# All cached value pages weighed on TensorE in four groups of PSUM rows, and head sums made from high and low parts

## The reference

```python
q, k, v, u, vc = split(rmsnorm(h, g_mix) @ w_in)        # 8 heads of 128 each
q, k = rmsnorm(q, g_q), rmsnorm(k, g_k)                 # per head
vc = layernorm(gelu(vc)); u = gelu(u)                   # per channel group of 128
z = q . k / sqrt(128) + bias_h                          # stick-breaking attention
A[t, s] = sigmoid(z[t, s]) * prod(s < j < t, 1 - sigmoid(z[t, j]))
o_sb = A @ v                                            # for a sample: 1024 cached values and weights
o_cm = u * (tril(W_s) @ vc + b)
h += concat(rmsnorm(o_sb), rmsnorm(o_cm)) @ w_out
h += (silu(rmsnorm(h) @ w_gate) * (rmsnorm(h) @ w_up)) @ w_down
h += sigmoid(rmsnorm(h) @ w_ple_gate) * (p @ w_ple_proj)
```

## Time and profile before

| | |
|---|---|
| median of 3 runs | 2385.37 us (2383.94 to 2385.87) |
| the profiled execution's own time | 2386.52 us |
| its span, first to last instruction | 2384.8 us |
| mean granted TensorE clock | 0.999 |
| busy: TensorE / VectorE / ScalarE / GpSimd | 99% / 75% / 51% / 16% |

### The profile page before, as it was taken

One profiled execution on the slowest core, in us unless ns is written; L12 is line 12 of the kernel. 1 busy time (PEld: TensorE's weight loads), 2 busy tenths in 40 slices (PEclk: granted clock), 3 DMA queues, 4 the chain that ended last, 5 costly groups with the idle time before them and its releaser, 6 DMA issues.

```text
span 2384.8 us, 46893 instructions
## 1 busy us (share of the span) xinstructions
PE 2359.9 (99%) x19392; PEld 2345.5 (98%) x19392; DVE 1788.7 (75%) x2196; ACT 1216.0 (51%) x1944; POOL 377.7 (16%) x364
## 2 busy tenths in 40 slices
PE   8999999999999989999999999999999999999999
PEld 8999999999999989999999999999999999999999
DVE  6369888886765598787888888888888887876333
ACT  6333445666743465555555646454646464545221
POOL 0001111111111300303030303030303030213000
PEclk9999999999999999999999999999999999999999
DMA  6256676564543533839393939384848474786323
GB/s 216 88 173 214 250 265 232 196 202 163 181 145 124 157 127 99 196 107 194 104 195 103 189 106 190 113 182 121 177 118 179 124 175 128 162 183 239 102 89 108
DMA packets 135734, 382.58 MB, mean 160 GB/s; under 512 B 14042, under 2 KB 58458, under 8 KB 126818
## 3 DMA queue, kind: packets, MB, share of 16 engines
q1 hardware_dynamic: 72594, 285.16, 35.7%
q0 software_dynamic: 62640, 94.28, 20.5%
q10 hardware_dynamic: 288, 0.14, 0.0%
HBM read 309.18 MB, written 73.55 MB: 160 GB/s over the span
## 4 chain that ended last, share of the span: by engine, by line
PE 90%; DVE 6%; DMA 2%; ACT 1%; issue 1%; SPq 0%; DVEq 0%; ACTq 0%
PE out_ps L2153 22%; PE tok_mix L2415 15%; PE pair_ps L2415 13%; PE out_ps L2488 10%; PE out_ps L2399 9%; PE out_ps L2415 8%; PE pair_ps L2488 5%; PE tok_mix L2488 2%; PE out_ps L2292 1%; PE pair_ps L2192 1%; DMA w_raw<-w_units 1%; DVE dot_s L1575 1%; DVE w_lo L1543 1%; DVE w_lo L1847 1%; DVE k_ring L1574 1%
## 5 line engine op out<-in xcount | busy, mean ns | idle before, releaser
L2153 PE MATMUL out_ps<-x_hi,w_hi 128*128 128x260 f32 x1792 | 376.0, 291 | 9.7 <-DVE w_lo L1692 7.8
L1314 ACT ACTIVATE w_hi<-w_sum 128x1024 fp32r<-128x1024 f32 (+1 forms) x252 | 215.5, 855 | 307.0 <-DVE w_sum L1859 210.3
L2153 PE MATMUL out_ps<-x_hi,w_lo 128*128 128x260 f32 x1792 | 361.5, 283 | 0.0
L2153 PE MATMUL out_ps<-x_lo,w_hi 128*128 128x260 f32 x1792 | 361.2, 283 | 0.0
L1314 ACT ACTIVATE w_hi<-w_raw 128x1024 fp32r<-128x1024 f32 (+1 forms) x306 | 261.4, 866 | 134.1 <-PE out_ps L2399 102.4
L1847 DVE TENSOR_TENSOR w_lo<-w_sum,w_hi 128x1024 fp32r<-128x1024 f32 (+1 forms) x252 | 244.5, 970 | 109.2 <-ACT w_hi L1314 108.6
L1001 POOL DMA_DIRECT2D h_dram<-staging x110 | 152.7, 1551 | 918.6 <-DVE staging L2008 900.4
L2415 PE MATMUL tok_mix<-op_hi,w_lo 128*128 128x260 f32 x1056 | 298.1, 282 | 0.0
L2415 PE MATMUL tok_mix<-op_lo,w_hi 128*128 128x260 f32 x1056 | 297.5, 282 | 0.0
L2415 PE MATMUL tok_mix<-op_hi,w_hi 128*128 128x260 f32 x1056 | 297.0, 281 | 0.0
L2153 PEld LDWEIGHTS out_ps<-x_hi,w_hi 128*128 128x128 f32 x1792 | 279.1, 189 | 12.7 <-DVE w_lo L1692 7.8
(11 more groups left out here) (341 smaller groups left out, 6162.5 us busy)
## 6 DMA issues: line engine op xcount, KB each, us to landing
w_raw<-w_units SPq DMA_DIRECT2D x239, 512.0 KB, 3.9
w_raw<-w_units SPq DMA_DIRECT2D x57, 1024.0 KB, 5.0
w_fifth<-w_units SPq DMA_DIRECT2D x58, 512.0 KB, 4.0
h_dram<-staging POOLq DMA_DIRECT2D x110, 260.0 KB, 6.8
k_ring<-cache_k SPq DMA_DIRECT2D x50, 512.0 KB, 4.8
v_ring<-cache_v POOLq DMA_DIRECT2D x42, 512.0 KB, 4.6
h_dram<-part POOLq DMA_DIRECT2D x50, 260.0 KB, 6.8
q_dram<-staging POOLq DMA_DIRECT2D x40, 260.0 KB, 6.9
```

Of the source, the lines that this page charges most:

```text
L1314: act.activation(dst, src, ACT.Copy).then_inc(hi_done, 1)
L2153: mm = pe.matmul(out_ps[:, 2 * (t % 2) + a, 0:HALF], w[:, u % 2, cols], x[:, a * HALF:(a + 1) * HALF], start=first and n == 0, stop=last a ...
```

## The change

Pages: the table by engines goes. All 64 pages are weighed by TensorE, in 25 units of two or three pages each, in one burst at b = 13. Operands change places: the one column of weights is now stationary and the values of a head (128 columns, f32) move, so that a head's result is one PSUM row of 128. Heads go in turn to rows 0, 32, 64 and 96 (twice, in two banks). After each burst VectorE copies or adds 256 columns of PSUM into `v_rows`, and once per sample TensorE turns the rows back with two matmuls by columns of `ident` (`turn_rows`, b = 9 of the next unit). ScalarE and VectorE no longer weigh or add pages.

Sums: after ScalarE squares a head it also copies it into an fp32r tile (`sq_hi`, which lies where `ug` or `k_head` lies), VectorE subtracts to get `sq_lo`, and TensorE sums both with four fp32r matmuls (`sum_parts`). The mean of vc is made likewise. `sq_hi` shares its place with `k_head`, so ScalarE now waits for `k_out` ahead of that copy. GpSimd's `add_squares` works in two halves, to make room.

```diff
-V_PLAN = v_plan()
-V_SUM = {21: (1, 14), 24: (2, 14), 29: (3, 14), 33: (4, 14), 36: (5, 14), 41: (6, 11), 45: (7, 14)}
+V_AT, TURN_AT = 13, 9
+V_UNIT_PAGES = ((0, 16, (3, 3, 2)), (1, 19, (2, 2, 2, 2)), (2, 23, (3, 3, 2)), (3, 26, (3, 3, 2)),
+                (4, 29, (3, 3, 2)), (5, 32, (3, 3, 2)), (6, 35, (3, 3, 2)), (7, 38, (3, 3, 2)))
+V_PLAN = [Page(first + i, 0) for _, first, counts in V_UNIT_PAGES for i, n in enumerate(counts) for _ in range(n)]
+V_PLAN = [Page(page.unit, j % V_SLOTS) for j, page in enumerate(V_PLAN)]
+ROW_AT = HALF + 2 * HEADS
...
+        def rows_ps(u):
+            first = 2 * ((tiles_before(u + 1) - 1) % 2)
+            return out_ps[:, first:first + 2, ROW_AT:ROW_AT + P]
+        def sq_hi(n):
+            return k_hi if n >= 2 * HEADS else ug_hi
...
 # ScalarE
                 act.activation(sq[:, :], src, ACT.Square).then_inc(sq_done, 1)
+                if n > 2 * HEADS:
+                    act.wait_ge(k_out, 16 * (n - 2 * HEADS))
+                act.wait_ge(sq_done, X_SQUARES + n + 1)
+                act.activation(sq_hi(n)[:, :], sq[:, :], ACT.Copy).then_inc(sq_hi_done, 1)
...
                     act.activation(vg[:, :], y[:, t % 2, :], ACT.Gelu).then_inc(gelu_done, 1)
+                    if i:
+                        act.wait_ge(cm_done, i)
+                    act.wait_ge(gelu_done, 2 * i + 1)
+                    act.activation(ug_hi[:, :], vg[:, :], ACT.Copy).then_inc(vg_hi_done, 1)
...
-                    weigh_pages(u)
...
 # VectorE
+            def low_sq(n):
+                dve.wait_ge(sq_hi_done, n + 1)
+                dve.tensor_tensor(sq_lo[:, :], sq[:, :], sq_hi(n)[:, :], ALU.subtract).then_inc(sq_lo_done, 1)
...
+                if u in V_TURN:
+                    dve.wait_ge(out_done, tiles_before(u + 1))
+                    dve.tensor_copy(q[:, :, PROMPT + V_TURN[u]], o_s_ps(u)).then_inc(v_read, 1)
+                if u in V_UNITS:
+                    ...
+                        dve.tensor_tensor(v_rows[:, :, :], v_rows[:, :, :], rows_ps(u), ALU.add).then_inc(rows_read, 1)
...
                     if u > U_KV + 1:
                         low_w(u + 1, 0)
                         low_w(u + 1, 1)
-                    pages_of(u, early=True)
+                    low_sq(2 * HEADS + i)
                     if i:
                         exponents(i - 1)
...
 # TensorE
+            def sum_parts(hi, lo, reader):
+                wait_free(pair_free, reader)
+                for x in (hi, lo):
+                    for a in range(2):
+                        mm = pe.matmul(pair_ps[:, a, 0:HALF], ones_r[:, :], x[:, a * HALF:(a + 1) * HALF],
+                                       start=x is hi, stop=x is lo)
+                return mm
...
+            def weigh_values(u):
+                pages = v_pages(u)
+                b = pages[0] // PAGES
+                pe.wait_ge(a_s_done, b + 1)
+                pe.wait_ge(rows_read, v_reads(u - 2))
+                for j in pages:
+                    pg = j % PAGES
+                    pe.wait_ge(v_in[V_PLAN[j].slot], 16 * (j // V_SLOTS + 1))
+                    for hd in range(HEADS):
+                        row, at = 32 * (hd % 4), pg * HEADS + hd
+                        mm = pe.matmul(rows_ps(u)[row:row + 1, hd // 4, :], a_s[:, b % 3, at:at + 1],
+                                       v_slot(j)[:, hd * P:(hd + 1) * P], start=False, stop=j == pages[-1],
+                                       skip_group_check=True)
+                    mm.then_inc(v_used, 1)
+            def turn_rows(u):
+                pe.wait_ge(rows_read, v_reads(u - 1))
+                pe.wait_ge(v_read, V_TURN[u])
+                for a in range(2):
+                    pe.matmul(o_s_ps(u)[:, 4 * a:4 * a + 4], v_rows[:, a, :], ident[:, 0:P:32],
+                              start=False, stop=True, skip_group_check=True)
```

More of the change, by code:

```diff
@@ L225 @@
 V_SLOTS = 3
[L226 to L291, removed]
@@ new lines @@
+Page = namedtuple("Page", "unit slot")
+V_UNIT_PAGES = ((0, 16, (3, 3, 2)), (1, 19, (2, 2, 2, 2)), (2, 23, (3, 3, 2)), (3, 26, (3, 3, 2)),
+                (4, 29, (3, 3, 2)), (5, 32, (3, 3, 2)), (6, 35, (3, 3, 2)), (7, 38, (3, 3, 2)))
+V_PLAN = [Page(first + i, 0) for _, first, counts in V_UNIT_PAGES for i, n in enumerate(counts) for _ in range(n)]
+V_PLAN = [Page(page.unit, j % V_SLOTS) for j, page in enumerate(V_PLAN)]
+V_LAST = {first + len(counts) - 1: b for b, first, counts in V_UNIT_PAGES}
@@ L353, with v_reads @@
+V_TURN = {u + 1: b for u, b in V_LAST.items()}
+V_UNITS = sorted({page.unit for page in V_PLAN})
+ROW_AT = HALF + 2 * HEADS
+def v_pages(u):
+    return [j for j, page in enumerate(V_PLAN) if page.unit == u]
+def v_reads(u):
+    return len([x for x in V_UNITS if x <= u])
 DIAG = lambda kb: slice(kb * P, (kb + 1) * P)
@@ L609, in build @@
         k_in = [sem(f"k_in{i}") for i in range(3)]
-        v_in = [sem(f"v_in{i}") for i in range(V_SLOTS + O_SLOTS)]
+        v_in = [sem(f"v_in{i}") for i in range(V_SLOTS)]
         q_rows_out = sem("q_rows_out")
@@ L2297, in sum_total @@
-            def sum_total(u, b):
-                first = v_first(b)
-                pe.wait_ge(v_added, adds_before(PAGES * (b + 1) - 1))
-                wait_sums(u)
-                for hd in range(HEADS):
-                    mm = pe.matmul(o_s_ps(u, b)[:, hd:hd + 1], v_slot(first)[:, hd * P:(hd + 1) * P], ones[:, 0:1],
-                                   start=False, stop=True, skip_group_check=True)
-                mm.then_inc(total_used, 1)
+            def weigh_values(u):
[12 more added lines that the diff above has]
+                    mm.then_inc(v_used, 1)
@@ L2332, in _ @@
                     i = (u - U_MLP - 1) // 2
[L2333 to L2334 removed]
+                    between[8] = lambda i=i: sum_values(i)
                 elif u <= U_KV:
@@ L2352, in _ @@
                         .then_inc(x_sum_ready, 1)
-                for j in v_pages(u):
-                    between[V_PLAN[j].at] = lambda j=j, u=u: weigh_values(j, u)
-                if u in V_SUM:
-                    between[V_SUM[u][1]] = lambda u=u: sum_total(u, V_SUM[u][0])
+                if u in V_UNITS:
+                    between[V_AT] = lambda u=u: weigh_values(u)
+                if u in V_TURN:
+                    between[TURN_AT] = lambda u=u: turn_rows(u)
                 if u - 1 in SUM_END:
```

184 lines of the change are left out of this document (61 added, 123 removed).

## The result

The changed kernel takes 2413.54 us (median of 4 runs, 2408.13 to 2415.07) against 2385.62 us for the kernel before on the same chip: ratio 1.0115, 95% interval 1.010 to 1.013. It is 1.2% slower; the forecast was 2376 us, in a range of 2361 to 2402. The profiled execution took 2412.01 us, with a span of 2410.4.

What follows compares the result with a forecast made beforehand. TensorE was taken as the bound, busy 2359.9 of 2384.8 us. Against 2386.5: -51.9 + 32.0 + 5.0 + 4.3 - 12.8 + 9 + 5 = -9.4, so 2377.1, median 2376 us; range 2361 to 2402.

Steps and rivals of the forecast that it cites:

- the terms of the forecast: TensorE's work: old page jobs -51.9 us, 64 new pages +32.0, 25 bursts +5.0, eight turns +4.3, 32 sums -12.8.
- near the side-by-side end: New pages on TensorE: four column groups stream nearly in parallel, 0.50 us a page (0.43 if fully), 64 pages 32.0 us.
- two at a time: Rival for new pages: records start strictly in order, two streams at most overlap, 0.85 us a page, 2394 us; chance 0.27.
- no overlap: Rival for new pages: products stream one after another, 1.70 us a page, 2445 us; chance 0.17.
- Sums: TensorE's head sums: four fp32r records replace plain f32, 0.40 us saved each, 32 sums 12.8 us, bounds 11 to 14.
- the new waits eat 14 of it: TensorE's added waiting: 9 us for k stores and 5 us for VectorE, against a gain of 23.4 from pages and sums.
- 9 for `k_out`: Sums in k units: TensorE waits for four late k stores, mean 2.2 us each, 9 us; 2 to 29 by landing time.
- a tighter VectorE: Units 16 to 23: VectorE busy 113.8 of TensorE's 114.6 us, so TensorE waits at the sums, 5 us, bounds 0 and 10.
- stores land late: Rival for k units: pages as forecast, but k stores take 11.2 us each, 20 us more, 2396 us; chance 0.05.

Runs made afterwards that it cites:

- pages alone: New pages with the old plain f32 sums, against the kernel before: 2376.08 us, ratio 0.9965.
- sums alone: Old pages with the new sums, the first k head's sum at block 7, against the kernel before: 2406.63 us, ratio 1.0102.
- pages, q sums: New pages, only the eight q heads' sums from high and low parts, all others plain; against the kernel before: 2371.96 us, ratio 0.9936.
- pages, q, k sums: Changed kernel with MLP heads' sums plain, k stores from ScalarE's queue, unit 25's low part ahead of the early key page: 2371.09 us, ratio 0.9944.
- best mix: The kernel of "pages, q, k sums" with VectorE scaling the MLP head before the early key page in even units 10 to 24: 2368.62 us, ratio 0.9931.
- k heads plain: Changed kernel with the eight k heads' sums in plain f32 as before, without copy or `k_out` wait on ScalarE: 2383.15 us, ratio 0.9992.
- k stores ScalarE: Changed kernel with each k store issued from ScalarE's queue instead of SP's, at the start of the unit behind: 2390.74 us, ratio 1.0024.
- unit 25 alone: The kernel of "k stores ScalarE" with the low part of the head's squares ahead of the early key page in unit 25: 2382.30 us, ratio 0.9990.
- later slots: Changed kernel, k stores from ScalarE, VectorE's low parts ahead of key pages, TensorE's MLP mean and turn two blocks later: 2385.93 us, ratio 1.0000.

## Why the prediction was wrong

**One account for all runs.** Take from each profiled span the waits of its view (from 40 to 840 or 850 us, up to the feed-forward part) and half of the time that TensorE was busy at half clock ahead of 850 us. What is left is what TensorE executes, and it should follow the terms of the forecast: 13.8 us less for the pages (-51.9 + 64 x 0.45 + 5.0 + 4.3, where 0.45 is my choice between 0.43 from page to page and 0.48 with the end of a burst shared out) and 0.40 less for each sum. Columns: span, waits, clock, rest, and the rest by these terms from the 2381.2 of before.

```
                           span   waits  clock   rest    by terms
before                    2384.8    3.6    0     2381.2     -
pages alone               2374.3    5.1   1.7    2367.5   2367.4
sums alone (32)           2398.9   23.2   6.4    2369.3   2368.4
pages, q sums (8)         2373.3    5.8   3.1    2364.4   2364.2
pages, q, k sums (16)     2367.4    5.5    0     2361.9   2361.0
best mix (16)             2367.6    5.1    0     2362.5   2361.0
k heads plain (24)        2379.9   16.8   5.0    2358.1   2357.8
k stores ScalarE (32)     2386.2   24.4   6.5    2355.3   2354.6
unit 25 alone (32)        2381.8   18.6   7.5    2355.7   2354.6
later slots (32)          2385.6   22.6   5.1    2357.9   2354.6
changed kernel (32)       2410.4   41.5  13.5    2355.4   2354.6
```

All agree within 1.5 us but one: the run with later slots has 3.3 us that this account does not name, and they stay open. The account is not sharper than some 2 us: with the half clock priced by the pace of pairs the changed kernel's rest is 1.4 higher, and with the three edges of the burst above (0.33 in all, 25 times) and 0.435 a page the pages save 11.5 instead of 13.8.

**Pages: right.** Forecast 0.50 a page, "near the side-by-side end"; measured 0.43 from page to page. That four heads share nothing but the issue was my reading; the runs show it by the time alone, 0.43 us with four rows against 1.74 with one. The rival "two at a time" asked for 0.85. It rested on TensorE starting its records strictly in order. The trace does not agree for these products: with the heads in the order 0, 4, 1, 5 four records start within 0.09 us (303.71 to 303.80), where on one row each follows the last after 0.109, and the burst takes 1.01 us instead of 0.98. The rival "no overlap" was worked out as 2445; with the plain sums of the run that made it happen (-12.8 + 9 left out) that is 2449, and 2452 was measured.

**Sums: right.** 0.40 each: 3.1 us between the rests of "pages" and "q sums", 12.1 us between those of "pages" and the changed kernel.

**What failed is the step on waits**, "the new waits eat 14 of it": 9 for `k_out` and 5 for a tighter VectorE. In its place TensorE waits 37.9 us more than before and loses 13.5 us to the clock behind the waits: 51.4 instead of 14. With 2.4 us more gained by pages and sums (-25.8, the difference of the two rests, instead of -23.4) this is 2377.1 + 37.4 - 2.4 = 2412.1, and the profiled execution took 2412.0. This sum closes by the way the rests are made; what tests it is the last column of the table. By parts:

- *`k_out`, 16.1 instead of 9.* The mechanism, the units and their number (four, none at 35 to 39) were right, and removing it was shown to pay. Only a size was off: from the issue to the copy it is 8.1 us in the mean, where the forecast took the median landing of all eight stores, 6.2.
- *Unit 25, 7.9 instead of nothing.* The forecast listed what is queued ahead of the sum for the k units with a store, and left out the first one, which has none. There the low part stands behind a key page that waits for its transfer. For ScalarE's new wait it asked what queues behind it, not what is ahead in the list of the engine that now makes the operand. Unit 25 alone shows it: 8.4 us by the medians, 4.4 by the spans of the two profiled executions.
- *MLP units, 17.3 instead of 5 (bounds 0 to 10).* The forecast made it a question of VectorE's busy time in units 16 to 23. The busy time came out about as forecast: 111.9 us in those units (222.3 to 351.3 us), where the forecast had 113.8. The waits did not: 10.6 us in those units, and 6.7 more in the MLP units ahead of them, for which the forecast had no term. It is a question of a chain: `ug` freed, copy, key page, subtraction, twice per head. The 16 MLP sums save 6.4 us and cost 11.2 net, by two runs measured apart (2383.15 and 2371.96). That VectorE is close to full there (three key pages ahead of the eviction) is argued from the timeline; no run took a key page away.
- *The clock, 13.5 instead of nothing.* The forecast had no term for it. The seven stretches at half clock begin in or right behind the seven waits of 2.96 us and more; the waits of 2.75, 2.3 and 2.1 us (units 17, 15, 29) have none. In other runs waits of 1.6 to 2.7 us had one (the pages alone: 2.7 us, then 320.3 to 323.7; the sums alone: 1.6, then 360.9 to 364.3), and one of 3.0 in the sums alone had none, so the length of a wait by itself does not decide it, and what does stays open. The kernel before shows the same once, at the entry of the feed-forward part, behind a wait of 4.1 us that ends at 859.9 (PEclk 0.75 from 859.8 to 866.6 us, 0.50 from there to 870.0). The seven stretches are 37.4 us long; half of their whole length would be 18.7 us. The account does not agree with this: the rest of the changed kernel would then be 2350.2, 4.4 us below its terms. It agrees with half of the 27.0 us in which TensorE was busy; in the other 10.4 us it waited, and a wait is counted once already.

So the rival "stores land late" was partly what happened (7 of the 37 us), and pages as forecast with almost four times the cost of waiting was in no rival. The range ended at 2402 because its upper end was set by dearer pages, not by dearer waits.

## What to carry to other kernels

When an operand is made in one more step on another engine, go through that engine's list in program order at every place where it is needed, the first and the last of each loop too, and ask what stands ahead of the new instruction and what that waits for; a busy share does not answer this. Where TensorE waits for some 3 us, look for the half clock behind it; here it was a third on top of the waits (13.5 us on 41.5). And try the halves of a change apart: here one half was worth 9 us, the other lost 22 alone and 37 on top of the first, and the part of the losing half whose chain is hidden was again a gain.

## What the runs showed of the hardware

- Plain f32 products with one stationary column each, spread over rows 0, 32, 64 and 96, took 0.43 us for eight heads of 128 columns against 1.74 on one row, a quarter. With neighbours in the program on the same row, a burst of two pages took 1.01 us instead of 0.98, and four of its records started within 0.09 us, where on one row each follows the last after 0.109: so they did not all start in the order of the program. A burst cost 0.09 us more in front, and 0.12 more in the block behind it.
- The granted clock fell from 1.00 to 0.50 to 0.51, for 3.4 or 6.8 us each, around all seven waits of 2.96 us and more in the changed kernel, whose TensorE was busy for 741 of the other 773 us from 40 to 850. In other runs one of 1.6 us had such a stretch and one of 3.0 had none. The 25 bursts of two or three pages did not lower it: in the best mix it is 1.00 from 40 to 840 us.
- The four k stores that SP issued 0.4 us behind a key page's load needed 5.3, 7.5, 9.3 and 10.3 us until ScalarE's copy could follow; one size, one queue, twice the time.
